# Eight first-table panels beside the making of the gates, and both halves of a route's keys in turn

## The chip, the cores and the metric

One core of one Trainium2 chip runs the whole kernel. The time is that of the device, in microseconds (us), from launch to end; the kernel before takes 3003.77 us, the median of three runs (3003.49 to 3005.74).

## The reference

Two transformer layers over 256 tokens of width 2048, all float32. The first is a convolution block with a SwiGLU; the second has forgetting attention with pooling, and then a layer of 128 x 128 = 16,384 tiny experts (PEER), which is the part that matters here:

```python
def peer(xn, w_query, sub_keys_1, sub_keys_2, expert_u, expert_v):
    q = (xt @ w_query).reshape(t, 8, 256)           # 8 heads
    s1, s2 = q1 . sub_keys_1, q2 . sub_keys_2       # 128 scores each
    v1, i1 = top_k(s1, 16); v2, i2 = top_k(s2, 16)
    cand = v1[..., :, None] + v2[..., None, :]      # 256 pairs
    top_s, top_pos = top_k(cand, 16)
    expert_idx = i1 * 128 + i2 at top_pos; gates = softmax(top_s)
    a = einsum('thkd,td->thk', expert_u[expert_idx], x)
    hid = gelu(a) * gates
    out = einsum('thk,thkd->td', hid, expert_v[expert_idx])
```

So each token takes 8 x 16 = 128 experts, each a row of 2048 floats in the first table (expert_u) and one in the second (expert_v).

## The kernel before

The first 1850 us (convolution, attention, matrix products) are not touched. The expert stage behind them computes the experts in two ways. Experts whose first key is below 88 are **gathered**: a *route* is one head of one half of the tokens (128 tokens, one a partition), 16 routes of 16 slots, in 64 *batches* of four slots. Experts whose first key is one of the last 40 (`DENSE = 40`) are computed **densely**: for each such key a *panel* of 128 experts (1 MB of the first table) is multiplied with all 256 tokens. Its Gelu is kept in `s_ha` (one block a panel), multiplied with gates that are zero where a token didn't choose the expert, and later multiplied with a panel of the second table.

What each engine does in batch g (its loop variable g or i):

- GpSimd issues the gathers, in one order for both tables: first-table row set k, then second-table row set k - 4 (`gather_u` L575, `gather_v` L588). There are 5 buffers for the first table (`s_u`), given back by VectorE's dots, and 7 for the second (`s_v`), given back by TensorE's adding.
- VectorE takes four dots (L1706, two halves each), then sums them (L1718, tile `s_adot`). After dot 0 it multiplies the last batch's activations with their gates (`hidden`, L1752). Batches 0 to 15 but every fifth (4, 9, 14) also carry the work of one route (`route`, L1688): the sixteen best keys of the first half behind dot 0, of the second behind dot 1 (`best_keys`, L1650), the best pairs behind dot 2, the experts' indices behind dot 3. `step` marks an instruction with a semaphore, `settled(back)` waits until all but the last `back` marked ones have ended, `link` does both at once.
- ScalarE makes the Gelu and spreads the activations (`spreads`, L1041) for TensorE, applies the Gelu to finished dense panels (`dense_hidden`, L1054) and, in batches 18 to 31, makes one-key matrices (`one_keys`, L1068).
- TensorE adds up the gathered rows of batch i - 1 (`adds`, L2284) and, in i = 0 to 16, runs the 40 first-table panels (`dense_u_panel`, L2228): three in each of the first two batches and some 2.3 in the others. Panel d goes to bank 4 + d % 4. In i = 18 to 31 it makes the gates, four tokens at a time ("fours", `token_four`, L2264), eight fours in batches 18 and 19 and four in the others, into banks 6 and 7. From i = 34 it runs the second-table panels.
- VectorE multiplies the gates onto `s_ha`, eight tokens of all 40 blocks at a time (`gated`, L1741), two fours behind TensorE.
- SyncE's queue loads the panels into two buffers (L468 to 479), each when the panel two before it is used. At d == DENSE it first waits until all first-table panels are used and then brings back two rows of tiles kept outside (`s_xn_late`, needed by the dots from batch 32 on, and `s_xres_late`, needed by TensorE at i = 33).

## Time and profile before

| | us |
|---|---|
| median of three runs | 3003.77 |
| the profiled execution | 3004.93 |
| its span, first to last instruction | 3002.9 |
| TensorE busy in it | 2736.4 |
| VectorE busy | 1923.8 |
| ScalarE busy | 1178.5 |
| GpSimd busy | 668.0 |

All stretches that are named in the text are in microseconds from the start of the span. PE is TensorE's matrix products, PEld its weight loads, DVE VectorE, ACT ScalarE, POOL GpSimd, SP SyncE. A share of busy time is an average over stages with different limits, so the text goes by stretches of the expert stage, from 1852 us to the end.

### The profile page before, as it was taken

How to read it: one execution, taken by the hardware profiler on the slowest of the kernel's cores; microseconds unless marked ns; L12 is line 12 of the kernel's file. 1: busy time of each engine (PE TensorE's matmuls, PEld its weight loads, DVE VectorE, ACT ScalarE, POOL GpSimd, SP SyncE). 2: the span in 40 equal slices, each digit the busy share in tenths (PEclk: the TensorE clock that was granted, in tenths of full speed). 3: DMA queues.
4: the chain of work that ended last, by engine and by line, in shares of the span. 5: the costliest groups of instructions: out<-in, count | busy, mean ns of one | idle time of the engine just before them, and what ended most of it. 6: DMA issues, size and time to landing. Idle time of an engine off the chain costs nothing.

```text
span 3002.9 us, 45413 instructions
## 1 busy us (share of the span) xinstructions
PE 2736.4 (91%) x17100; PEld 2038.3 (68%) x17100; DVE 1923.8 (64%) x3184; ACT 1178.5 (39%) x2298; POOL 668.0 (22%) x568
## 2 busy tenths in 40 slices
PE   8999999999999998999999999999976678888884
PEld 7886788888888887989999889777753322222220
DVE  6888566555656565455445558987769875555555
ACT  1003443334333344425334444645456642222232
POOL 0000000000000000040000002544448765454453
PEclk9999999999999998999999999999977779999886
DMA  6333545555555553443555657999999999999997
GB/s 244 140 141 111 206 157 185 187 191 183 194 182 193 184 192 122 155 152 141 182 182 182 248 199 250 372 418 408 415 375 408 397 409 417 409 420 391 411 409 300
DMA packets 131297, 785.51 MB, mean 262 GB/s; under 512 B 34630, under 2 KB 34630, under 8 KB 35846
## 3 DMA queue, kind: packets, MB, share of 16 engines
q1 hardware_dynamic: 55424, 393.68, 35.5%
q0 software_dynamic: 75712, 389.74, 32.3%
q8 instruction: 93, 1.52, 0.2%
q14 instruction: 68, 0.56, 0.1%
HBM read 940.23 MB, written 4.19 MB: 315 GB/s over the span
## 4 chain that ended last, share of the span: by engine, by line
PE 57%; DMA 20%; DVE 12%; issue 6%; ACT 3%; POOL 1%; DVEq 1%; POOLq 0%; SPq 0%; ACTq 0%
DMA s_u<-in_expert_u,s_u_index 17%; PE bank L1847 10%; PE bank L1841 10%; PE bank L1843 10%; PE bank L1842 10%; PE bank L1848 5%; PE bank L1937 4%; DVE s_u L1706 4%; PE bank L2240 4%; PE bank L2292 2%; DMA s_v<-in_expert_v,s_v_index 2%; DVE s_cacc L1217 2%; ACT s_spread L1050 2%; DVE s_w_lo L1128 1%; DVE s_yrow L1390 1%
## 5 line engine op out<-in xcount | busy, mean ns | idle before, releaser
L1128 DVE TENSOR_TENSOR s_w_lo<-s_raw,s_w_hi 128x2048 fp32r<-128x2048 f32 x258 | 592.6, 2297 | 577.8 <-ACT s_w_hi L628 577.4
L628 ACT ACTIVATE s_w_hi<-s_raw 128x2048 fp32r<-128x2048 f32 x256 | 490.5, 1916 | 750.9 <-PE bank L1843 475.4
L1847 PE MATMUL bank<-s_a,s_w_hi 128*128 128x512 f32 x1408 | 494.7, 394 | 3.2 <-DVE s_w_lo L1128 3.2
L2292 PE MATMUL bank<-s_v,s_spread 128*32 128x512 f32 x2048 | 302.8, 721 | 183.1 <-ACT s_spread L1050 115.9
L1706 DVE CUSTOM_DVE_ANT_0 s_u<-s_u,s_xn_late 128x1024 f32<-128x1024 f32 x256 | 303.8, 1224 | 246.8 <-DMA s_u<-in_expert_u,s_u_index 246.5
L1050 ACT ACTIVATE s_spread<-s_ident,s_hid 32x32 f32<-32x32 f32 x1024 | 325.6, 318 | 205.5 <-DVE s_hid L1756 188.0
L1848 PE MATMUL bank<-s_a,s_w_lo 128*128 128x256 f32 x1408 | 395.1, 281 | 0.0
L585 POOL DMA_INDIRECT s_u<-in_expert_u,s_u_index x256 | 300.0, 1172 | 416.4 <-DVE s_halfdot L1706 240.4
L601 POOL DMA_INDIRECT s_v<-in_expert_v,s_v_index x256 | 317.9, 1242 | 196.8 <-PE bank L2292 115.5
L1706 DVE CUSTOM_DVE_ANT_0 s_u<-s_u,s_xn 128x1024 f32<-128x1024 f32 x256 | 303.8, 1224 | 60.3 <-DMA s_u<-in_expert_u,s_u_index 59.3
L1841 PE MATMUL bank<-s_a,s_w_hi 128*128 128x256 f32 x1152 | 325.1, 282 | 3.4 <-DVE s_a L1152 1.8
L1842 PE MATMUL bank<-s_a,s_w_hi 128*128 128x256 f32 x1152 | 324.4, 282 | 0.0
L1843 PE MATMUL bank<-s_a,s_w_lo 128*128 128x256 f32 x1152 | 324.0, 281 | 0.0
L2292 PEld LDWEIGHTS bank<-s_v,s_spread 128*32 128x32 f32 x2048 | 62.9, 125 | 375.5 <-ACT s_spread L1050 135.4
L1847 PEld LDWEIGHTS bank<-s_a,s_w_hi 128*128 128x128 f32 x1408 | 264.7, 188 | 66.5 <-DVE s_w_lo L1128 6.4
L2250 PE MATMUL bank<-s_raw,s_ha 128*32 128x512 f32 x2560 | 295.5, 615 | 0.0
L2240 PE MATMUL bank<-s_xnt,s_raw 128*128 128x256 f32 x1184 | 264.7, 382 | 2.1 <-DMA s_raw<-in_dense_u 2.1
L1848 PEld LDWEIGHTS bank<-s_a,s_w_lo 128*128 128x128 f32 x1408 | 265.0, 188 | 0.4
L2240 PEld LDWEIGHTS bank<-s_xnt,s_raw 128*128 128x128 f32 x1184 | 222.1, 190 | 58.7 <-issue 29.1
L1937 PE MATMUL bank<-s_a_f,s_raw 128*128 128x272 f32 x1024 | 235.2, 393 | 2.9 <-DVE s_a_f L1185 2.1
L2250 PEld LDWEIGHTS bank<-s_raw,s_ha 128*32 128x32 f32 x2560 | 83.3, 115 | 215.1 <-issue 215.1
L1937 PEld LDWEIGHTS bank<-s_a_f,s_raw 128*128 128x128 f32 x1024 | 194.4, 190 | 43.4 <-issue 3.5
(321 smaller groups left out, 3809.8 us busy)
## 6 DMA issues: line engine op xcount, KB each, us to landing
s_raw<-in_stream SPq DMA_DIRECT2D x292, 1024.0 KB, 4.7
s_raw<-in_expert_v SPq DMA_DIRECT2D x40, 1024.0 KB, 8.9
s_raw<-in_dense_u SPq DMA_DIRECT2D x37, 1024.0 KB, 8.7
s_u<-in_expert_u,s_u_index POOLq DMA_INDIRECT x256, 17.4
s_v<-in_expert_v,s_v_index POOLq DMA_INDIRECT x256, 17.6
s_panel_early<-in_dense_u POOLq DMA_DIRECT2D x3, 1024.0 KB, 11.5
s_xres<-in_x SPq DMA_DIRECT2D x2, 1024.0 KB, 6.0
out<-s_out_row SPq DMA_DIRECT2D x32, 64.0 KB, 3.3
```

The costliest lines, as they stand in the source:

```text
L628: act.activation(w_hi[s % 2][:, :], raw[s][:, :], ACT.Copy).then_inc(hi_ready, 1)
L1050: ins = act.activation(spread[g % NW][s * Q:(s + 1) * Q, q, :], ident[own, own], ACT.Copy, scale=hid[g % NH][own, s:s + 1])
L1128: dve.tensor_tensor(w_lo[s % 2][:, :], raw[s][:, :], w_hi[s % 2][:, :].bitcast(f32), ALU.subtract)\
L1706: ins = dve.tensor_tensor_reduce(out=u_slot[k % NU][:, half], in0=u_slot[k % NU][:, half], in1=xn_late[:, half] if t else xn[:, 0, half], ...
L1841: pe.matmul(dst, left[0], right[0], start=start, stop=False)
L1842: pe.matmul(dst, left[0], right[1], start=False, stop=False)
L1843: return pe.matmul(dst, left[1], right[0], start=False, stop=stop)
L1847: pe.matmul(dst, left[0], both, start=start, stop=False)
L1848: return pe.matmul(dst[:, 0:T], left[1], both[:, 0], start=False, stop=stop)
L1937: ins = pe.matmul(bank[c][:, 0:L], raw[c % 4][:, k * 128:(k + 1) * 128], a_f[:, k, :], start=k == 0, stop=k == KT - 1)
L2240: ins = pe.matmul(bank[b][:, 0:T], source[:, k * 128:(k + 1) * 128], xnt[:, k, 0:T], start=k == 0, stop=k == KT - 1)
L2292: ins = pe.matmul(bank[4 * t + q][c * Q:(c + 1) * Q, :], spread[g % NW][:, q, :], v_slot[k % NV][:, c * 512:(c + 1) * 512], start=False, s ...
```

## The change

Of the forty first-table panels 32 (`FIRST_U`) pass in batches 0 to 16, one or two in each from the first on, and 8 (`LATE_U`) while the gates are made: panel 32 at i = 18, then one each at i = 20, 21, 23, 25, 26, 28 and 29, at the head of TensorE's work of the batch. They use banks 4 and 5. A late panel misses the gates of the tokens before it. So `gated` copies the gates of the missing blocks into `s_ha` as they are; ScalarE puts the Gelu of the tokens already gated into a new tile (`s_late_act`, on the place of `s_pick` and `s_cand`, which the routes no longer need) and that of the others into `s_ha`; and VectorE multiplies the two in a new step, `landed`, two batches after the panel (batches 20, 22, 23, 25, 27, 28, 30, 31, with 48 to 224 tokens). SyncE's code is the same, but its wait for all forty panels now ends at i = 29.

The keys of both halves of a route are found behind dot 0 with their instructions in turn (`best_keys_of_both`), so that a step waits for one that is not the last. The pairs move behind dot 1, the indices behind dot 2.

```diff
+FIRST_U, LATE_U = 32, 8
...
-    return d + 16 if d < 24 else d - 16 if d < 32 else d - 32
+    return d + 16 if d < 24 else d - 16 if d < FIRST_U else DENSE - 1 - d
...
 def u_panels_in(i):
 
-    if i < 2:
-        return range(3 * i, 3 * i + 3)
-    return range(6 + 34 * (i - 2) // 15, 6 + 34 * (i - 1) // 15) if i < 17 else range(0)
+    if i < 17:
+        return range(FIRST_U * i // 17, FIRST_U * (i + 1) // 17)
+    return range(FIRST_U + LATE_U * (i - 17) // 13, FIRST_U + LATE_U * (i - 16) // 13) if i < 30 else range(0)
+
+
+def u_bank(d):
+
+    if d < FIRST_U:
+        return 4 + d % 4, d // 4
+    return 4 + (d - FIRST_U) % 2, FIRST_U // 4 + (d - FIRST_U) // 2
+
+
+def gated_before(g):
+
+    fours = 8 * (g - 18) if g < 20 else 4 * (g - 16)
+    return max(0, min(fours, T // 4) // 2 - 2)
+
+
+LANDS_IN = {d: i + 2 for i in range(30) for d in u_panels_in(i) if d >= FIRST_U}
...
+    late_act = place("s_late_act", [128, 2, T], pick_at)
...
             def dense_hidden(d):
 
-                b = 4 + d % 4
+                b, late = u_bank(d)[0], d - FIRST_U
                 act.wait_ge(panel_used, NPANELS + 1 + d + 1)
-                if d == 32:
-                    act.wait_ge(expert_ready, PH)
-                act.activation(ha[:, dense_block(d), :], bank[b][:, 0:T], ACT.Gelu_apprx_tanh).then_inc(bank_empty[b], 1)
+                done = 0
+                if late >= 0:
+                    done = GATE_TOKENS * gated_before(LANDS_IN[d])
+                    if late == 0:
+                        act.wait_ge(expert_ready, TT * PH)
+                    wait(act, late_landed, late - 1)
+                    act.activation(late_act[:, late % 2, 0:done], bank[b][:, 0:done], ACT.Gelu_apprx_tanh)
+                act.activation(ha[:, dense_block(d), done:], bank[b][:, done:T], ACT.Gelu_apprx_tanh).then_inc(bank_empty[b], 1)
...
+            def best_keys_of_both(th):
+
+                values = [val[:, half * TOPK:(half + 1) * TOPK] for half in range(2)]
+                indices = [ind[:, half * TOPK:(half + 1) * TOPK] for half in range(2)]
+                src = [score[:, score_row(th), half * NKEYS:(half + 1) * NKEYS] for half in range(2)]
+                rest = [sc_rest[:, :], cand_rest[:, 0:NKEYS]]
+                for h in range(2):
+                    apart()
+                    step(dve.max(values[h][:, 0:8], src[h]))
+                for h in range(2):
+                    settled(1 + h)
+                    apart()
+                    step(dve.max_index(indices[h][:, 0:8], values[h][:, 0:8], src[h]))
+                    step(dve.match_replace(rest[h], values[h][:, 0:8], src[h], LOWEST))
+                for h in range(2):
+                    settled(2 - h)
+                    apart()
+                    step(dve.max(values[h][:, 8:16], rest[h]))
+                for h in range(2):
+                    settled(1)
+                    apart()
+                    step(dve.max_index(indices[h][:, 8:16], values[h][:, 8:16], rest[h]))
+                settled()
...
             def route(th, turn):
 
-                if turn < 2:
-                    best_keys(th, turn)
+                if turn == 0:
+                    best_keys_of_both(th)
+                elif turn == 1:
+                    best_pairs()
                 elif turn == 2:
-                    best_pairs()
-                else:
                     pairs_experts(th)
...
-            def gated(group):
+            def gated(group, missing):
 
                 b = 6 + group % 2
                 if group == 0:
                     for a in range(2):
-                        dve.wait_ge(bank_empty[4 + a], n.after(f"empty{4 + a}", DENSE // 4))
+                        dve.wait_ge(bank_empty[4 + a], n.after(f"empty{4 + a}", FIRST_U // 4))
                 dve.wait_ge(one_key_used, GATE_TOKENS // 4 * (group + 1))
                 some = ha[:, :, GATE_TOKENS * group:GATE_TOKENS * (group + 1)]
-                dve.tensor_tensor(some, some, bank[b][:, 0:GATE_TOKENS * DENSE].rearrange("p (t g) -> p g t", t=GATE_TOKENS), ALU.mult)\
-                    .then_inc(bank_empty[b], 1)
+                gates = bank[b][:, 0:GATE_TOKENS * DENSE].rearrange("p (t g) -> p g t", t=GATE_TOKENS)
+                if missing:
+                    dve.tensor_copy(some[:, 0:missing, :], gates[:, 0:missing, :])
+                dve.tensor_tensor(some[:, missing:, :], some[:, missing:, :], gates[:, missing:, :], ALU.mult).then_inc(bank_empty[b], 1)
+
+            def landed(d):
+
+                late, (b, k) = d - FIRST_U, u_bank(d)
+                groups = gated_before(LANDS_IN[d])
+                for group in (groups - 2, groups - 1):
+                    gates_taken = n.after(f"empty{6 + group % 2}", FIRST_U // 4 + 2 + group // 2)
+                    dve.wait_ge(bank_empty[6 + group % 2], gates_taken)
+                dve.wait_ge(bank_empty[b], n.after(f"empty{b}", k + 1))
+                some = ha[:, dense_block(d), 0:GATE_TOKENS * groups]
+                dve.tensor_tensor(some, some, late_act[:, late % 2, 0:GATE_TOKENS * groups], ALU.mult).then_inc(late_landed, 1)
...
-                    fours = token_fours_in(g)
+                    for d in range(FIRST_U, DENSE):
+                        if turn == 0 and LANDS_IN[d] == g:
+                            landed(d)
+                    fours, missing = token_fours_in(g), sum(LANDS_IN[d] > g for d in range(FIRST_U, DENSE))
                     for f in fours[turn * len(fours) // 4:(turn + 1) * len(fours) // 4]:
                         if f >= 4 and f % 2 == 0:
-                            gated(f // 2 - 2)
+                            gated(f // 2 - 2, missing)
...
             def dense_u_panel(d):
 
-                b = 4 + d % 4
+                b, k = u_bank(d)
                 if d == 0:
                     pe.wait_ge(xnt_ready, 1)
-                into(b, d // 4)
+                into(b, k)
```

Counts of buffers' uses (`DENSE // 4` becomes `FIRST_U // 4`, and for banks 4 and 5 at i = 33 `FIRST_U // 4 + LATE_U // 2`) follow in the same way.

## Rows read from the trace of the kernel before

**Rows 1.** the page's parts 2 and 3: DMA tenths, GB/s in 40 slices, gathers' queue

```profile
DMA  6333545555555553443555657999999999999997
GB/s 244 140 141 111 206 157 185 187 191 183 194 182 193 184 192 122 155 152 141 182 182 182 248 199 250 372 418 408 415 375 408 397 409 417 409 420 391 411 409 300
...
q0 software_dynamic: 75712, 389.74, 32.3%
```

**Rows 2.** windows: length, busy us (instructions) by engine, granted clock, DMA share, GB/s

```profile
1852.00:1912.00 60.00, 57.62 (x292) 45.26 (x282) 54.44 (x160) 26.93 (x87) 22.18 (x21) 1.00 0.84 305
1912.00:2186.00 274.00, 272.49 (x1445) 198.19 (x1444) 222.10 (x615) 152.44 (x490) 134.39 (x112) 1.00 1.01 414
2186.00:2251.00 65.00, 46.49 (x273) 32.15 (x271) 43.52 (x81) 32.23 (x96) 28.03 (x25) 0.74 0.92 371
2251.00:2450.00 199.00, 134.61 (x890) 68.18 (x893) 179.48 (x337) 118.44 (x358) 148.53 (x112) 0.73 1.00 402
2450.00:2985.00 535.00, 423.13 (x3527) 111.40 (x3519) 294.93 (x543) 158.82 (x510) 272.27 (x237) 0.88 0.99 405
1960.00:1980.00 20.00, 20.00 (x108) 14.65 (x107) 18.20 (x55) 12.16 (x40) 10.14 (x9) 1.00 1.02 424
```

**Rows 3.** waits, 1852 to 2200 us: total us, times, longest

```profile
POOL s_v L601 <- PE bank L2292: 80.6, 25, 9.8
...
DVE s_u L1706 <- DMA s_u<-in_expert_u,s_u_index: 39.1, 20, 3.9
```

**Rows 4.** groups by line, 1852 to 2200 us: count | busy, mean ns | idle before

```profile
L2240 PE MATMUL bank<-s_xnt,s_raw 128*128 128x256 f32 x1184 | 264.7, 382 | 2.1 <-DMA s_raw<-in_dense_u 2.1
...
L2292 PE MATMUL bank<-s_v,s_spread 128*32 128x512 f32 x512 | 61.6, 598 | 1.8 <-ACT s_spread L1050 1.8
```

**Rows 5.** timeline of DVE: sums that end batches 2, 3 and 4; start, duration in us

```profile
1911.78 0.15 DVE L1718 TENSOR_TENSOR s_adot<-s_halfdot 128x4 f32<-128x4 f32 x1
...
1931.85 0.15 DVE L1718 TENSOR_TENSOR s_adot<-s_halfdot 128x4 f32<-128x4 f32 x1
...
1941.83 0.17 DVE L1718 TENSOR_TENSOR s_adot<-s_halfdot 128x4 f32<-128x4 f32 x1
```

**Rows 6.** timeline of DVE: one half of a route's keys before, start and duration

```profile
1894.74 0.29 DVE L1639 MAX8 s_val<-s_score 128x8 f32<-128x128 f32 x1
1895.18 0.09 DVE L1641 MATCH_VALUE_LOAD s_ind<-s_val,s_score 128x8 f32 x1
1895.26 0.28 DVE L1641 FIND_INDEX8 s_ind<-s_val,s_score 128x8 uint32<-128x128 f32 x1
1895.46 0.07 DVE L1642 MATCH_VALUE_LOAD s_sc_rest<-s_val,s_score 128x8 f32 x1
...
1896.78 1.22 DVE L1706 CUSTOM_DVE_ANT_0 s_u<-s_u,s_xn 128x1024 f32<-128x1024 f32 x1
```

**Rows 7.** timeline of PE: fours (L2280) and adding (L2292), idle time in brackets

```profile
2216.85 3.71 PE L2280 MATMUL bank<-s_one_key,s_one_key 128*128 128x40 f32 x16 [12.63 <-ACT s_one_key L1082]
...
2223.90 5.50 PE L2292 MATMUL bank<-s_v,s_spread 128*32 128x512 f32 x32
...
2245.79 4.80 PE L2292 MATMUL bank<-s_v,s_spread 128*32 128x512 f32 x32
...
2285.16 5.59 PE L2292 MATMUL bank<-s_v,s_spread 128*32 128x512 f32 x32 [4.21 <-ACT s_spread L1050]
2290.68 1.98 PE L2280 MATMUL bank<-s_one_key,s_one_key 128*128 128x40 f32 x16
```

**Rows 8.** DMA issues and median landing: 1852:1912, 1945:2186, 2345:2450

```profile
s_u<-in_expert_u,s_u_index POOLq DMA_INDIRECT x12, 8.6
...
s_u<-in_expert_u,s_u_index POOLq DMA_INDIRECT x48, 19.9
...
s_u<-in_expert_u,s_u_index POOLq DMA_INDIRECT x29, 14.9
```

**Rows 9.** groups by line and shape, 2186 to 2450 us

```profile
L1749 DVE TENSOR_TENSOR s_ha<-s_ha,bank 128x320 f32<-128x320 f32 x32 | 15.4, 481 | 3.2 <-PE bank L2280 3.2
```

More of the change, by code:

```diff
@@ L442, in two_layers @@
         spread_ready, v_used = sem("spread_ready"), sem("v_used")
+        late_landed = sem("late_landed")
         acc_done, out_ready, stored = sem("acc_done"), sem("out_ready"), sem("stored")
@@ L1082, in one_keys @@
                 act.activation(four, four, ACT.Relu, scale=-1.0, bias=1.0).then_inc(one_key_ready, 1)
-            slots_stored = [n.after(f"empty{6 + t}", DENSE // 4 + 1) for t in range(TT)]
+            slots_stored = [n.after(f"empty{6 + t}", FIRST_U // 4 + 1) for t in range(TT)]
             for g in range(ROUTES * GROUPS):
@@ L1723, in one_keys_2 @@
                     for t in range(TT):
-                        dve.wait_ge(bank_empty[6 + t], n.after(f"empty{6 + t}", DENSE // 4 + 1))
+                        dve.wait_ge(bank_empty[6 + t], n.after(f"empty{6 + t}", FIRST_U // 4 + 1))
                 wait(dve, one_key_used, 2 * (m - 2))
@@ L1815, in _ @@
                     if g == 32 and turn < 2:
-                        gated(T // GATE_TOKENS - 2 + turn)
+                        gated(T // GATE_TOKENS - 2 + turn, 0)
                 dots_summed(g)
@@ L2258, in slots_transposed @@
                 pe.wait_ge(gates_ready, PH * (t + 1))
-                into(6 + t, DENSE // 4)
+                into(6 + t, FIRST_U // 4)
                 for kind in range(3):
@@ L2267, in token_four @@
                 if f % 2 == 0:
-                    into(b, DENSE // 4 + 1 + f // 4)
+                    into(b, FIRST_U // 4 + 1 + f // 4)
                 turn = 2 * (f // 4) + f % 4
@@ L2309, in _ @@
                     for b in (4, 5):
-                        into(b, DENSE // 4)
+                        into(b, FIRST_U // 4 + LATE_U // 2)
                     for b in (6, 7):
-                        into(b, DENSE // 4 + 1 + T // GATE_TOKENS // 2)
+                        into(b, FIRST_U // 4 + 1 + T // GATE_TOKENS // 2)
                     pe.wait_ge(xres_back, 16)
```

## Prediction

> **What bounds the kernel now.** I read the page first: the DMA's busy tenths and rate over time, and what the gathers moved [rows 1]. The change touches only the last part of the kernel, the expert stage, which starts near 1852 us. There the DMA row stands at 9 in nearly every slice and the rate near 410 GB/s. So the stage is first of all bound by bytes; the question is where the DMA engines are *not* full. Second, I cut the stage into five stretches [rows 2]. The last column is the rate (five rows; the sixth is one window of 20 us): 305 GB/s in the first 60 us (the first three batches), 414 up to 2186, 371 while the one-key machinery starts, 402 while the gates are made, 405 after that. Times the lengths this is 18.3, 113.4, 24.1 and 80.0 MB for the first four. Third, the waits of the first two stretches [rows 3]: VectorE waited 39.1 us for gathered rows of the first table, and the queue of GpSimd, which issues all gathers in order, waited 80.6 us for TensorE to give back buffers of the second table. TensorE's work there is 37 first-table panels in 264.7 us, 7.15 us each, with hardly any idle time in front (2.1 us), three more like them, and 61.6 us of adding, 3.85 a batch [rows 4]: 40 x 7.15 + 61.6 = 348 us, all there is from 1852 to 2200. So up to batch 16 TensorE and the DMA are both full. The first batches have a third limit: the sums of two routed batches lie 20.07 us apart (1911.78, 1931.85), the next, without a route, takes 9.98 [rows 5], and a gather lands in 8.6 us against 19.9 later [rows 8]: VectorE sets the pace and the DMA has room. While the gates are made a gather takes 14.9 us [rows 8]: nearly full, not quite.
>
> **The profiled execution** spans 3002.9 us and took 3004.93; the median is 3003.77. I change the profiled stretches and take the difference from the median.
>
> **The change, part by part.**
>
> *Alternating the halves.* Before, each half of a route's keys is a chain in which every step but one waits for the instruction just before it: four waits a half, eight a route. From the first maximum (1894.74) to the next dot (1896.78) one half takes 2.04 us [rows 6]; two take 4.08. An instruction behind a wait starts 0.15 us after the end of the one before (0.29 us from 1894.74, then 1895.18); one without a wait starts 0.08 before it (1895.46 against 1895.54) [rows 6]. After the change seven of the eight waits look one or more instructions further back. At 0.23 each I walk the new order to about 2.65 us for both halves, 1.4 saved per route; bounds are 0 (the waits aren't what holds it) and 1.6. A routed batch then costs VectorE 18.7 us instead of 20.07. Only where VectorE sets the pace does this shorten the kernel: three batches in the first stretch, 3 x 1.4 = **4.2 us** (0 to 4.8). Pairs and experts move one dot earlier; the indices are used batches later, nothing there is late.
> The row shows 0.23 us between a waiting and a free instruction. The Trainium skill ("VectorE: DVE Perf Modes", the section on the DRAIN you can't avoid) says that the next operation starts only when the pipeline is empty and that the semaphore costs nothing extra, so that only the number of operations counts. By that rule alternation saves nothing; that is a rival below. The trace disagrees, with starts 0.08 us ahead of the end.
>
> *Eight panels leave the first 17 batches.* TensorE loses 8 x 7.15 = 57 us of work there and is no longer the limit. Per five batches (four routed) it then has 9.4 x 7.15 + 5 x 3.85 = 86 us, VectorE 4 x 18.7 + 10 = 85, so the DMA should lead. Loads run two panels ahead, so by the end of batch 16 they are at panel 33 instead of 39: six loads of 1.05 MB fewer, two of them in the first stretch (where the DMA isn't the limit), four in the second. 113.4 - 4.2 = 109.2 MB. At which rate? 414 GB/s was reached beside a TensorE that held buffers back; single windows reach 424 [rows 2]. I take 418: 261 us instead of 274, **13 us** saved. Bounds: 405 GB/s, the rate of the last stretch [rows 2], gives 270 (4 saved), 422 gives 259 (15). The first batches get one or two panels instead of three; their adding waits for ScalarE's copies, not for TensorE, and TensorE idles some microseconds, which costs nothing there.
>
> *Batches 17 to 19.* SyncE's queue loads the two rows kept outside (tile xn_late and xres_late) and the first two second-table panels once all forty panels are used. That was at the start of this stretch, 4.2 MB in 10 us of DMA time; now it comes after panel 39, in batch 29. One or two late panels (1.0 MB) take its place: 24.1 - 4.2 + 1.0 = 20.9 MB, 50 us at 414. VectorE has 43.5 us here [rows 2] plus about 1.5. What else bounds it is the chain sum, spread, one-keys, eight fours, adding: 21.9 us for batch 19 with hardly a wait for gathers in it (adding starts at 2223.90, 2245.79) [rows 7]. Batch 17 has 389.7/64 = 6.1 MB of gathers [rows 1], 15.5 us. With two batches of 20 to 21 behind it this is 57 us for 65, **8 us** saved (bounds 4 and 13, the latter with VectorE and DMA alone). Panel 32 stands ahead of the first fours of batch 18, in the 12.63 us in which TensorE waited for ScalarE [rows 7]: free, as long as that wait is longer than the panel. VectorE has gates only for those landed; the chain isn't longer.
>
> *The gates, batches 20 to 33.* Added on VectorE: 28 small copies and 8 products of 48 to 224 columns. Neither is in the trace; the copies move 8 to 64 elements a row, between the 155 ns of a four-column sum [rows 5] and the 481 ns of the 320-column gate product [rows 9]. Near the lower end: 28 x 0.17 + 8 x 0.28 = 7 us, less 1.5 for the shorter gate products, 5.5 (bounds 3 and 12). VectorE had 179 of 199 us; 185 stays under what the DMA needs. The waits in front of a landing are for instructions a batch old. ScalarE: two Gelu instead of none, 0.8 us a panel beside 118 us in 199. The DMA: 80.0 + 4.2 (moved here) + 5.2 (five late panels) = 89.4 MB. At 402, the present rate, 222 us; at 422, 212. The present rate is one of 12 slots in flight with no plain loads beside them; with loads beside them the gathers took 19.9 us and the rate was 414 [rows 2, 8], so I take 415: 215.4 us instead of 199, **16.4 us** lost (bounds 13 and 23). The loads moved here are due at batch 32 (xn_late), three batches after the issue, some 40 us against a landing of at most 20 [rows 8].
> TensorE: seven panels stand ahead of the adding, which now waits 4.2 us for ScalarE [rows 7]. A panel of 7.15 us passes 2.9 us on. Behind it the GpSimd queue stands with a gather of the second table, and behind that the next gather of the first, which VectorE needs. With 14.9 us in flight, I expect 2.9 us to be covered.
>
> *After batch 33* nothing is changed: same bytes, same order, same panels in hand.
>
> **Sum:** -4.2 - 13 - 8 + 16.4 = -8.8 us: **2995 us**. Best ends together: -4.8 - 15 - 13 + 13 = -20; worst: 0 - 4 - 4 + 23 = +15.
>
> **Rivals.**
> *The alternation gives nothing* (the drain rule). Routed batches stay at 20.07: the first stretch saves nothing, the second has 10 x 20.07 + 4 batches of some 16 = 265, 9 saved. -9 - 8 + 16.4 = -0.6, **3003 us**. Against it: the overlapping starts in [rows 6].
> *Bytes alone.* The same megabytes are moved; where the gates are made the DMA runs at 402 again (+23), the rest as forecast: -2, **3002 us**. For it: a DMA share of 1.00 at 402 [rows 2].
> *The DMA never starves.* Panels fill the weak stretches, rates of 422 in both long stretches, and batches 17 to 19 in 53 us: -4.2 - 15 - 12 + 13 = -18, **2986 us**. For it: 371 and 305 GB/s are there to be filled.
> *TensorE becomes the bound while the gates are made (slower).* Its granted clock is 0.73 on average in that stretch [rows 2], between the levels of 1.2 and 2.4 GHz, as it idles 4 us in every batch; the same adding takes 5.59 us there [rows 7] against 3.85 [rows 4]. If the panels run at 1.2 GHz, 14.3 us each, TensorE has 14 x 9.4 (adding and fours, [rows 7]) + 7 x 14.3 = 232 us, over the 215 of the DMA: +32 instead of +16.4, **3011 us**. It decides when the seven panels take more than (215 - 132)/7 = 12 us each. Against it: the panels fill just the idle time before which the clock fell, and the fours, which run right behind the adding, have full speed (1.98 us for 16 [rows 7], 3.71 after a gap).
> The Trainium skill ("TensorE: Matmul & The Clock Gate", Part 1) says that an idle TensorE falls to half clock and a busy one returns; the trace agrees with it, and it speaks on both sides: for slow panels behind a gap, against gaps once they are filled.
>
> **How the numbers follow.** Forecast 0.42; alternation empty 0.17; bytes alone 0.10; never starving 0.17; TensorE bound 0.14. What a measurement of this kernel can tell from no change is about 0.2%, 6 us, so faster means under 2997.8. The forecast's own spread (2989 to 3001) lies on that side with 0.36 of its 0.42; with the never-starving case 0.53 faster. The two middle rivals and the rest of the forecast are 0.33 same; 0.14 slower. The range leaves out the outer part of the best and of the slower case: 2984 to 3008.
>
> **What would show it.** Right: sums of the first routed batches 18.7 us apart; the dot of batch 16 ending near 2168; TensorE with some 8% idle before that; a rate of 415 or more in the gate stretch and its end (sum of batch 33) at about 2441 instead of 2450; panels of about 7.2 us there. Wrong: routed batches still 20 us apart; gather times under 15 us between 1930 and 2168 (then something else than the DMA holds it); GpSimd waiting long for TensorE between 2226 and 2441; the first dots of batch 32 waiting for xn_late.

## The result: 10 us slower

| | before | after |
|---|---|---|
| median, seven runs each in turn | 3005.16 us | 3015.01 us |
| lowest to highest | 3003.49 to 3008.86 | 3012.25 to 3017.70 |
| span of the profiled execution | 3002.9 | 3013.0 |

After over before: 1.0034, 95% interval 1.0025 to 1.0044. Forecast were 2995 us and a range of 2984 to 3008; the kernel is slower by more than the 0.2% that can be told.

The page of the kernel after: span, granted clock, DMA tenths, GB/s in 40 slices of the span.

```profile
span 3013.0 us, 45458 instructions
...
PEclk9999999999999999999999999999988778998886
DMA  6343545555555553444545657999989999999997
GB/s 243 140 141 111 209 154 188 188 183 193 183 193 183 193 181 130 154 147 143 186 181 182 250 196 255 370 415 408 412 330 419 385 417 417 411 420 394 413 407 303
```

Against [rows 1]: where batches 17 to 19 run there is now a slice of 330 GB/s (before 375). The same five stretches as [rows 2], cut at the same events (the ends of VectorE's sums of batches 2, 16, 19 and 33); columns as there: length, busy us of PE, PEld, DVE, ACT, POOL, granted clock, DMA share, GB/s.

```profile
1852.00:1908.00 56.00, 41.95 (x206) 30.56 (x199) 53.10 (x159) 26.05 (x83) 20.69 (x20) 0.85 0.77 275
1908.00:2174.00 266.00, 250.04 (x1301) 174.06 (x1300) 216.82 (x615) 150.39 (x484) 122.21 (x112) 0.96 1.01 412
2174.00:2238.00 64.00, 48.16 (x266) 32.26 (x268) 43.69 (x88) 32.33 (x97) 30.91 (x25) 0.76 0.86 334
2238.00:2461.00 223.00, 180.32 (x1132) 112.77 (x1128) 183.27 (x367) 121.72 (x372) 143.15 (x112) 0.80 0.99 401
2461.00:2996.00 535.00, 423.22 (x3528) 110.75 (x3520) 295.45 (x548) 159.16 (x512) 266.01 (x237) 0.88 0.99 406
```

The ends of the last three sums that cut it (line, tile, start, duration):

```profile
2173.93 0.16 DVE L1766 TENSOR_TENSOR s_adot<-s_halfdot 128x4 f32<-128x4 f32 x1
...
2237.83 0.16 DVE L1766 TENSOR_TENSOR s_adot<-s_halfdot 128x4 f32<-128x4 f32 x1
...
2461.05 0.16 DVE L1766 TENSOR_TENSOR s_adot<-s_halfdot 128x4 f32<-128x4 f32 x1
```

Every kernel of this study was cut in the same way. All later sections read from this table; a time is the length of the stretch in that kernel's trace, "rest" runs to the end of its span, and the last two columns are of timed runs, 5 to 11 of each (the kernel before, timed beside them, took 3004.3 to 3005.5 us). One of its runs took 4581.89 us at a granted clock of 0.554 and is in no median or ratio here. Each kernel has one trace, and the seven that are the same program up to batch 16 (after, late_no_loads, spread_loads, late_two, fours_half, panels_behind, panels_last) end that batch between 2173.1 and 2176.0: 2 or 3 us in one stretch can be chance.

| kernel | up to batch 2, ends at | batches 3 to 16 | 17 to 19 | 20 to 33 | rest | median | ratio, 95% |
|---|---|---|---|---|---|---|---|
| before | 1911.8 | 273.7 | 65.2 | 199.3 | 552.9 | 3005.16 | |
| after | 1907.5 | 266.4 | 63.9 | 223.2 | 552.0 | 3015.01 | 1.0034 (1.0025–1.0044) |
| keys_only | 1907.4 | 275.7 | 64.7 | 199.7 | 553.4 | 3004.07 | 0.9996 (0.9987–1.0005) |
| panels_only | 1912.3 | 261.7 | 64.8 | 221.9 | 552.5 | 3015.89 | 1.0034 (1.0021–1.0048) |
| before_late_loads | 1912.0 | 272.1 | 63.7 | 209.1 | 553.3 | 3012.20 | 1.0026 (1.0016–1.0036) |
| late_no_loads | 1907.2 | 266.2 | 62.9 | 210.2 | 554.0 | 3002.51 | 0.9990 (0.9981–0.9999) |
| spread_loads | 1907.9 | 266.0 | 63.9 | 221.7 | 555.0 | 3016.48 | 1.0036 (1.0023–1.0050) |
| late_two | 1907.2 | 265.9 | 64.6 | 222.2 | 550.5 | 3013.01 | 1.0027 (1.0016–1.0037) |
| fours_half | 1909.9 | 266.1 | 58.7 | 222.6 | 551.0 | 3008.78 | 1.0009 (1.0000–1.0018) |
| front_loaded | 1907.7 | 260.7 | 66.2 | 223.1 | 552.1 | 3013.19 | 1.0028 (1.0016–1.0040) |
| even40 | 1910.6 | 276.5 | 68.0 | 199.4 | 553.5 | 3010.39 | 1.0017 (1.0008–1.0026) |
| two_in_gap | 1908.6 | 272.2 | 68.6 | 199.9 | 552.1 | 3003.27 | 0.9994 (0.9985–1.0003) |
| panels_behind | 1907.7 | 266.5 | 63.3 | 222.9 | 555.2 | 3019.71 | 1.0050 (1.0036–1.0063) |
| panels_last | 1907.8 | 266.7 | 61.6 | 225.7 | 554.2 | 3018.29 | 1.0046 (1.0032–1.0059) |

So the sum that was forecast as -4.2 - 13 - 8 + 16.4 = -8.8 came out as -4.3 - 7.3 - 1.3 + 23.9 - 0.9 = +10.1 us. Three terms missed by some 6 to 8 us each, all to the same side.

### The profile page after: what moved, and what is told of

Same layout as the page of the kernel before. It is cut to its first block, busy times and chain, and to the rows that moved or that the text cites. A ratio compares the mean times of both kernels' runs of the same rounds, so it can differ in the third digit from the quotient of the medians.

```text
span 3013.0 us, 45458 instructions
## 1 busy us (share of the span) xinstructions
PE 2745.7 (91%) x17100; PEld 2043.8 (68%) x17100; DVE 1921.4 (64%) x3220; ACT 1179.0 (39%) x2306; POOL 645.9 (21%) x568
## 4 chain that ended last, share of the span: by engine, by line
PE 59%; DMA 19%; DVE 11%; issue 5%; ACT 4%; DVEq 1%; POOL 1%; POOLq 0%; SPq 0%; ACTq 0%
DMA s_u<-in_expert_u,s_u_index 16%; PE bank L1911 10%; PE bank L1905 10%; PE bank L1906 10%; PE bank L1907 10%; PE bank L1912 5%; PE bank L2001 4%; PE bank L2304 4%; DVE s_u L1754 3%; PE bank L2356 3%; DMA s_v<-in_expert_v,s_v_index 3%; PE bank L2314 2%; DVE s_cacc L1241 2%; ACT s_spread L1069 2%; PE bank L2344 1%
## 5 line engine op out<-in xcount | busy, mean ns | idle before, releaser
L604 POOL DMA_INDIRECT s_u<-in_expert_u,s_u_index x256 | 290.4, 1134 | 505.3 <-DVE s_halfdot L1754 318.4
L620 POOL DMA_INDIRECT s_v<-in_expert_v,s_v_index x256 | 305.3, 1193 | 140.3 <-issue 76.9
L2304 PE MATMUL bank<-s_xnt,s_raw 128*128 128x256 f32 x1184 | 271.5, 388 | 0.0
L2304 PEld LDWEIGHTS bank<-s_xnt,s_raw 128*128 128x128 f32 x1184 | 226.5, 194 | 58.0 <-issue 27.6
## 6 DMA issues: line engine op xcount, KB each, us to landing
s_panel_early<-in_dense_u POOLq DMA_DIRECT2D x3, 1024.0 KB, 11.6
```

The costliest lines, as they stand in the source:

```text
L2304: ins = pe.matmul(bank[b][:, 0:T], source[:, k * 128:(k + 1) * 128], xnt[:, k, 0:T], start=k == 0, stop=k == KT - 1)
```

## The experiments

The theories at stake: the *bytes* decide where the gates are made (a moved load costs its DMA time), or TensorE's work, or where that work stands; and in batches 17 to 19 a *chain* of engines decides and loads ride along for nothing, or the bytes do.

### One half of the change alone

**keys_only** is the kernel before with the new keys.

```diff
-                if turn < 2:
-                    best_keys(th, turn)
+                if turn == 0:
+                    best_keys_of_both(th)
+                elif turn == 1:
```

> The kernel before with the alternation alone; all forty panels stay in the first 17 batches. Theory A (TensorE sets the first 17 batches there, VectorE only the first three): the first batches' sums lie 18.7 us apart instead of 20.07, but the stretch to batch 16 ends where it did (2185, within 2 us), as TensorE's 348 us of work are untouched; total 3005, within 3 us. Rival: the alternation is worth its full 4.2 us or more on its own: sum of batch 16 at 2181 or earlier, total 3001 or less.

**panels_only** is the kernel after with the old keys (this edit the other way).

> The changed kernel with the keys of a route in the old order (half after half, each instruction waiting for the last). If the alternation shortens every routed batch that TensorE no longer sets: sums of routed batches 20.1 us apart throughout, batch 16 ends at 2179 to 2182 instead of 2174, total 3019 to 3023. Rival (the DMA sets the stretch after 1930, so only the first batches lose): batch 16 ends at 2177 to 2179, total 3016 to 3019. If the drain rule held and the waits cost nothing: no change, 3014 to 3016.

Measured: 3004.07 and 3015.89 us. The loss is all the panels'. The new keys are as fast as forecast: VectorE of the kernel after, one route (start, duration):

```profile
1872.86 0.49 DVE L1688 MAX8 s_val<-s_score 128x8 f32<-128x128 f32 x2
1873.30 0.09 DVE L1692 MATCH_VALUE_LOAD s_ind<-s_val,s_score 128x8 f32 x1
...
1874.35 0.29 DVE L1697 MAX8 s_val<-s_sc_rest 128x8 f32<-128x128 f32 x1
1874.58 0.29 DVE L1697 MAX8 s_val<-s_cand_rest 128x8 f32<-128x128 f32 x1
1874.79 0.08 DVE L1701 MATCH_VALUE_LOAD s_ind<-s_val,s_sc_rest 128x8 f32 x1
...
1875.44 1.23 DVE L1754 CUSTOM_DVE_ANT_0 s_u<-s_u,s_xn 128x1024 f32<-128x1024 f32 x1
```

Both halves take 1875.44 - 1872.86 = 2.58 us instead of 4.08 [rows 6]: 1.5 saved (1.4 forecast). Yet keys_only ends batch 2 4.4 us early and then takes 2.0 us more for batches 3 to 16, ending batch 16 at 2183.1 instead of 2185.5; with the panels moved as well nothing of it is left at batch 16, 2174.0 without it and 2173.9 with it. Its timed gain, 0.9996, can't be told from none.

panels_only came out as neither of its first two theories: it ends batch 16 at 2174.0, not at 2177 or later, and the total is that of "no change", though for another reason than the one given there, since the keys do take longer. Where the time goes is seen in the batches. Batches 11 to 13, with a route each, take 60.5 us in it and 56.3 in the kernel after; batch 14, without one, takes 12.1 in it and 18.7 after. What VectorE saves in routed batches it waits in the next one. And up to batch 2 panels_only had moved 60 x 0.267 = 16.0 MB where the kernel after had moved 56 x 0.275 = 15.4.

### Loads moved into the gates, and loads taken out of them

**before_late_loads** is the kernel before, except that SyncE holds back the four plain loads behind the panels (4.2 MB) until batch 27 has been added up; nothing else moves.

```diff
                     sp.wait_ge(panel_used, NPANELS + 1 + DENSE)
+                    sp.wait_ge(v_used, 4 * 28)
```

> The kernel before, but the four loads of 1.05 MB (the two rows kept outside and the first two second-table panels) wait until the adding of batch 27 is done, as they in effect do in the changed kernel. Theory L (these loads were free at batches 17 to 19, where the chain of one-keys, fours and adding sets the pace and the DMA has room, and cost their DMA time where the gates are made): batches 17 to 19 take 62 to 65 us instead of 65, batches 20 to 33 take 207 to 211 instead of 199, total 3011 to 3015: the whole loss of the change. Rival (late panels alone do the harm): batches 17 to 19 gain what the others lose, total within 3 us of 3005.

**late_no_loads** is the kernel after without the loads of the last six late panels (6.3 MB, 5.8 of them where the gates are made, by the windows below); TensorE multiplies what lies in the buffers, so the result is another. (The count of loads that the second-table panels wait for follows.)

```diff
+                if FIRST_U + 2 <= d < DENSE:
+                    continue
...
-                else:
+                elif d < FIRST_U + 2:
                     pe.wait_ge(raw_loaded[(d - NE) % 2], (NPANELS // 4 + (d - NE) // 2 + 1) * 16)
```

> The changed kernel without the loads of its last six late panels (TensorE multiplies what lies in the buffers, so the result is another; all instructions stay). Theory bytes: 6.3 MB fewer, one load of them at batches 17 to 19 (no gain there: the chain sets the pace) and five where the gates are made, at 2.4 us each: batches 20 to 33 take 209 to 213 us instead of 223, total 3001 to 3005. Theory TensorE or VectorE (the panels' work, not their bytes): within 3 us of 3015.

**late_two** is the kernel after with the loads, but only 2 of 16 products of each late panel.

```diff
-                for k in range(KT):
+                for k in range(KT) if d < FIRST_U else (0, KT - 1):
```

> The changed kernel, with each of the eight late panels multiplied in 2 steps of 16 instead of all (part of the sum is left out): TensorE has 0.9 us of work for such a panel instead of 7.15, all transfers and all work of the other engines stay. If the panels ahead of the adding do the harm, because the adding gives buffers back late and the queue of GpSimd stands (theory TensorE): batches 20 to 33 take 212 to 216 us instead of 223, total 3004 to 3008. If bytes set that stretch (theory bytes): 221 to 224, total 3013 to 3016.

Windows of batches 17 to 19 and 20 to 33 of the three, in this order, columns as above:

```profile
2184.00:2248.00 64.00, 47.89 (x277) 33.20 (x275) 43.58 (x84) 32.33 (x97) 30.67 (x26) 0.76 0.83 323
2248.00:2457.00 209.00, 140.66 (x888) 71.22 (x891) 180.09 (x338) 118.56 (x358) 146.36 (x112) 0.70 1.00 403
```

```profile
2173.00:2236.00 63.00, 46.49 (x262) 30.08 (x261) 43.66 (x88) 32.35 (x97) 30.18 (x24) 0.78 0.85 322
2236.00:2446.00 210.00, 178.61 (x1112) 115.63 (x1112) 182.48 (x368) 121.76 (x372) 148.11 (x112) 0.81 0.99 398
```

```profile
2173.00:2238.00 65.00, 41.06 (x230) 25.76 (x232) 43.85 (x90) 32.47 (x98) 30.48 (x25) 0.71 0.84 329
2238.00:2460.00 222.00, 158.44 (x928) 86.39 (x924) 183.41 (x368) 121.60 (x372) 142.75 (x112) 0.71 1.00 403
```

The second line of each gives the megabytes: 209 x 0.403 = 84.2, 210 x 0.398 = 83.6, 222 x 0.403 = 89.5; before it was 80.0 and after 223 x 0.401 = 89.4. Time follows bytes, at 398 to 403 GB/s, and nothing else in these lines: late_no_loads does all the work of the kernel after on every engine and takes 13 us less; late_two takes 22 us off TensorE (158 for 180) and gets 1 us, and 2 us in all. All three stretches lie where the theories of bytes had put them (207 to 211, 209 to 213 and 221 to 224 us). Four loads cost before_late_loads 9.8 us there (2.45 each) and some 7 us in all; without six of them the kernel after is 12.5 us faster.

The first line of each tells the second thing. The kernel before moved 24.1 MB in this stretch and took 65.2 us; before_late_loads moved 64 x 0.323 = 20.7 MB and took 63.7. Taking 3.4 MB away saved 1.5 us, which is within chance, and not the 8.5 that they would take at 402 GB/s.

### Is it the burst, or where the panels stand?

**spread_loads** lets the four loads go one after another instead of together behind panel 39.

```diff
+                    sp.wait_ge(v_used, 4 * 30)
...
+                if d >= DENSE and d < DENSE + 2:
+                    sp.wait_ge(v_used, 4 * (31 + d - DENSE))
```

(The first stands before the load of xres_late.)

> The changed kernel, with the four loads no longer issued at once behind panel 39 but the first at once and the others one a batch from the adding of batch 29 on. If it is their coming in one burst that starves the dots and the adding near 2400 (theory burst): batch 30 takes 15 to 16 us instead of 21.2 and the total falls by 4 to 8 us to 3007 to 3011. If their bytes are what costs (theory bytes): batches 30 to 34 share the same loss, total 3013 to 3017.

No gain: 221.7 us there, but 3 us more in the rest, 3016.48 in all. Batch 30 does fall from 21.2 to 13.7 us, as the theory of the burst has it, but batch 29 grows from 17.1 to 21.5 and batches 32 and 33 by 4.4 together: the bytes' time only moves.

Next, one place in the kernel after fitted the forecast's own warning sign, GpSimd waiting for TensorE. GpSimd's issues (start, duration, idle time before and who ended it):

```profile
2375.11 1.10 POOL L604 DMA_INDIRECT s_u<-in_expert_u,s_u_index  x1 [0.30 <-issue]
2381.13 1.99 POOL L620 DMA_INDIRECT s_v<-in_expert_v,s_v_index  x1 [4.92 <-PE bank L2356]
```

TensorE had begun the panel ahead of that batch's adding at 2369.84, and the DMA's rate over 2370 to 2400, in 40 slices, shows the hole:

```profile
GB/s 372 426 426 350 371 306 415 339 295 361 361 350 350 372 186 186 109 66 197 251 448 284 262 295 339 371 393 437 415 361 426 295 426 393 404 426 371 481 371 459
```

It falls to 66 GB/s near 2383 us, and the mean of these 30 us is 344. **panels_behind** puts the late panels of batches 20 to 29 behind the adding, **panels_last** behind the fours too.

```diff
-                for d in u_panels_in(i)[:1]:
+                for d in u_panels_in(i)[:1] if i < 20 else ():
                     dense_u_panel(d)
...
-                for d in u_panels_in(i)[2:]:
+                for d in u_panels_in(i)[2 if i < 20 else 0:]:
                     dense_u_panel(d)
```

> The kernel after, with the seven late panels of batches 20 to 29 behind TensorE's adding of their batch and ahead of its fours, instead of ahead of both. The computation is whole. In the trace of the kernel after the rate falls from some 420 GB/s to 66 to 250 between 2379 and 2385 us, right behind a late panel of 9.41 us (2369.84), while GpSimd waits 4.92 us for TensorE to give back a buffer of the second table; from 2370 to 2400 the rate is 344 GB/s. Theory A (a late panel at the head of TensorE's work holds buffers back, and that is the missing rate): the dip is gone, GpSimd's waits for TensorE between 2238 and 2461 (17.3 us in the kernel after) fall, the stretch of batches 20 to 33 takes 223 - 5 = 218 us, total near 3010. Theory B (the bytes set the end, a dip is made up by the buffers in hand or by others elsewhere): the stretch stays at 222 to 223 us, total 3013 to 3016. Theory C (the fours are now late, and VectorE's gate products wait for them): over 225 us.

> As the kernel panels_behind, with the late panels of batches 20 to 29 behind the fours of their batch, so that neither the adding nor the fours of the batch wait for them; a panel can hold only the next batch's adding, which waits for ScalarE's copies in any case. The computation is whole. Theory A: 217 to 218 us for batches 20 to 33, total near 3009 to 3010, and no dip of the rate under 300 GB/s near 2380. Theory B: 222 to 223 us, total 3013 to 3016, the same as panels_behind. Theory C: under panels_behind by what its gate products waited for TensorE.

Neither is faster: 3019.71 and 3018.29 us, read as slower than the kernel after by 3 to 5, though the intervals of the ratios overlap. No theory had the totals right; the stretch of panels_behind is that of theory B (222.9 us), the one of panels_last is over B's and A's (225.7). The hole moves: the rate of panels_behind falls to 142 GB/s near 2394, that of panels_last to 229 near 2400. The waits of panels_behind between 2238 and 2465 (total us, times, longest):

```profile
POOL s_u L604 <- PE bank L2356: 27.7, 7, 7.3
...
DVE s_ha L1799 <- PE bank L2344: 25.7, 8, 6.5
```

The same of the kernel after, 2238 to 2461:

```profile
POOL s_u L604 <- PE bank L2356: 9.6, 6, 5.6
POOL s_v L620 <- PE bank L2356: 7.7, 4, 4.9
DVE s_ha L1799 <- PE bank L2344: 6.9, 5, 3.0
```

GpSimd waits for TensorE 27.7 us in front of the first table's gathers (after 17.3 in front of both tables'), and VectorE 25.7 us for gates (after 6.9). So these two runs put other waits in the place of the first, and what the hole itself costs they can't show. The stretch takes 222.9 us again with 88.4 MB (89.3 after), and the rest is 3 us longer.

late_two shows it, because there the panel at the head is nearly gone. Its rate over the same 30 us, 2370 to 2400:

```profile
GB/s 437 382 415 426 339 317 350 393 382 382 404 339 459 317 426 361 306 361 317 361 306 371 339 382 437 393 459 393 404 437 382 459 415 448 393 448 426 404 448 404
```

No slice is under 306 GB/s and the mean is 391, yet the stretch takes 222.2 us for 223.2. The hole is gone and the time isn't: the theory that the place at the head costs the missing rate falls.

### What bounds batches 17 to 19

**fours_half** is the kernel after with the products of two of the four tokens in each of the first sixteen fours (those of batches 18 and 19), so half of these gates are left out.

```diff
-                for e in range(4):
+                for e in ((0, 3) if f < 16 else range(4)):
```

> The changed kernel with two of four tokens in each of the first sixteen fours (batches 18 and 19; half of these gates are left out). Theory chain (batches 17 to 19 are set by sum, spread, one-keys, fours, adding, one behind the other, the first fours at half clock): TensorE's 7.3 + 3.9 us of fours a batch are halved, batches 18 and 19 take 19 to 21 us instead of 23.7 and 22.4, together 4 to 8 us less, and total 3008 to 3012. Rival (VectorE's own work or the gathers set them): within 2 us of 3015.

TensorE of the kernel after in this stretch (start, duration, idle before):

```profile
2192.72 7.17 PE L2304 MATMUL bank<-s_xnt,s_raw 128*128 128x256 f32 x32
...
2225.84 3.71 PE L2344 MATMUL bank<-s_one_key,s_one_key 128*128 128x40 f32 x16 [6.31 <-ACT s_one_key L1106]
2229.35 3.61 PE L2344 MATMUL bank<-s_one_key,s_one_key_late 128*128 128x40 f32 x16
2232.90 6.09 PE L2356 MATMUL bank<-s_v,s_spread 128*32 128x512 f32 x32
```

TensorE waits 6.31 us for ScalarE's one-keys, then runs 16 small products in 3.71 us where 1.98 is its time at full clock [rows 7]; the granted clock of the stretch is 0.76, a mean of its two levels, 1.2 and 2.4 GHz. (The Trainium skill, "TensorE: Matmul & The Clock Gate", Part 1, has a TensorE that sat idle at half clock; the row agrees.) Behind them stands the adding, and GpSimd waits for it, 15.8 us in this stretch. The same stretch of fours_half (columns as above):

```profile
2176.00:2235.00 59.00, 37.99 (x214) 22.02 (x212) 43.67 (x88) 32.49 (x98) 33.18 (x25) 0.80 0.92 358
```

With half of these products it takes 58.7 us instead of 63.9 (batches 18 and 19: 21.2 and 19.8 for 23.7 and 22.4), at 358 GB/s instead of 334 and nearly the same bytes, and the kernel 3008.78 us instead of 3015.01: the chain over these engines sets this stretch, and time taken out of it reaches the end. Batch 19 shows the chain most plainly: it takes 22.41 or 22.42 us in all nine kernels with late panels and whole fours, and 21.81 to 21.89 in before, keys_only and before_late_loads. The half microsecond between them fits ScalarE's two Gelu of the late panel, which stand right ahead of its one-keys in the kernel after (2223.33 to 2223.78); that was not tried by itself.

The room has an end. even40 and two_in_gap (below) move 26.3 and 25.7 MB in this stretch and take 68.0 and 68.6 us. Whether bytes cost that, or in two_in_gap the two panels, was not tried.

### How the first seventeen batches share the panels

**front_loaded** is the kernel after with three panels in each of the first two batches, as before, and 26 in the others.

```diff
+    if i < 2:
+        return range(3 * i, 3 * i + 3)
     if i < 17:
-        return range(FIRST_U * i // 17, FIRST_U * (i + 1) // 17)
+        return range(6 + 26 * (i - 2) // 15, 6 + 26 * (i - 1) // 15)
```

> The changed kernel with three panels again in each of the first two batches and 26 spread over the next fifteen; the eight late panels stay. Theory free room (before about 1930 the DMA isn't full because VectorE sets the pace, so the loads drawn there are free, and the even distribution gives two of them up): the stretch up to batch 16 has 2.1 MB less to move when the DMA is full, batch 16 ends at 2168 to 2171 instead of 2174, total 3009 to 3013. Rival (the sum of bytes up to batch 16 alone decides, wherever they lie): batch 16 at 2173 to 2175, total 3014 to 3016.

**even40** is the kernel before with its forty panels spread evenly.

```diff
-    if i < 2:
-        return range(3 * i, 3 * i + 3)
-    return range(6 + 34 * (i - 2) // 15, 6 + 34 * (i - 1) // 15) if i < 17 else range(0)
+    return range(DENSE * i // 17, DENSE * (i + 1) // 17) if i < 17 else range(0)
```

> The kernel before with its forty panels spread evenly over the first 17 batches (two or three in each), nothing late, keys in the old order. Theory TensorE (it sets that stretch with 348 us of work, and every gap it gets in the first two batches moves the end): it runs out of panels before the adding of batch 1 and idles 5 to 8 us, batch 16 ends at 2189 to 2194 instead of 2185, total 3009 to 3013. Rival (the DMA alone sets that stretch): batch 16 within 2 us of 2185, total 3003 to 3007.

The first two stretches of front_loaded:

```profile
1852.00:1908.00 56.00, 55.18 (x280) 43.61 (x276) 53.05 (x159) 26.91 (x86) 18.98 (x19) 1.00 0.84 303
1908.00:2168.00 260.00, 233.98 (x1223) 158.28 (x1216) 216.31 (x613) 149.75 (x482) 123.94 (x113) 0.93 1.00 409
```

It moves 303 GB/s in the first 56 us, where the kernel after moves 275: 1.6 MB more, in the same time. Batch 16 ends 5.5 us earlier (2168.4 against 2173.9). Of that 2.3 us go again in batches 17 to 19 (66.2 for 63.9), and 3013.19 is only 1.8 under 3015.01, which their intervals don't tell apart: batch 16 ended where theory free room had it, the total did not. even40 loses 5 to 6 us on before (1.0017): batch 16 ends 1.6 us later, where the rival had it, and batches 17 to 19 take 2.8 more, so that the total is the one of theory TensorE. TensorE, which has the same forty panels to do up to batch 16, sits idle 8.64 us early on for want of ScalarE's copies (in the kernel before 1.76, at 1882.48). That this is what costs it was not tried by itself.

```profile
1881.25 3.64 PE L2290 MATMUL bank<-s_v,s_spread 128*32 128x512 f32 x16 [8.64 <-ACT s_spread L1048]
```

### Only what fits the gap

**two_in_gap** moves two panels instead of eight, to batches 17 and 18, where TensorE waits for ScalarE, and keeps three in each of the first two batches (panel 38 stands behind the adding of i = 17). It has the new keys.

```diff
-FIRST_U, LATE_U = 32, 8
+FIRST_U, LATE_U = 38, 2
...
+    if i < 2:
+        return range(3 * i, 3 * i + 3)
     if i < 17:
-        return range(FIRST_U * i // 17, FIRST_U * (i + 1) // 17)
-    return range(FIRST_U + LATE_U * (i - 17) // 13, FIRST_U + LATE_U * (i - 16) // 13) if i < 30 else range(0)
+        return range(6 + 32 * (i - 2) // 15, 6 + 32 * (i - 1) // 15)
+    return range(21 + i, 22 + i) if i < 19 else range(0)
```

(The counts of buffers' uses follow.)

> Another distribution, with the alternation: 38 panels in the first 17 batches, three in each of the first two as before, one behind the adding of batch 17 and one at the head of batch 18, in the 12.6 us in which TensorE waits for the one-keys. The four loads of kept rows and second-table panels then follow at about 2215, still where the DMA has room. Theory free room: nothing is moved to where the gates are made, TensorE has 14 us less before; the first 17 batches end 3 to 6 us earlier than 2185, the rest stays: total 2998 to 3002, faster than the kernel before. Rival (the DMA's bytes up to batch 16 are the same 37 loads, so nothing is gained): 3003 to 3006.

Measured 3003.27 us, ratio 0.9994 with 1 inside its interval: the total of the rival, not the 2998 to 3002 of theory free room. It wins 4.7 us up to batch 16 (2180.8 for 2185.5), loses 3.4 in the next three (68.6 for 65.2), and pays nothing in the gates. It beats the kernel after by 12 us and the kernel before by nothing that can be told.

## Why the prediction was wrong, step by step

**The alternation, -4.2.** Right in its own place (-4.3; routed batches end 18.69 us apart, 1869.83 and 1888.52, for 18.7). The rival that it saves nothing is refuted, and with it the reading of the drain rule that the prediction weighed (the Trainium skill, "VectorE: DVE Perf Modes", The DRAIN you can't avoid): 2.58 us for 4.08, with as many instructions. (The same section of the Trainium skill adds that an operation that isn't held starts earlier; the row agrees, with 1895.46 against an end at 1895.54 [rows 6].) The step that failed is the sum: the gain of the first three batches was added to the one of batches 3 to 16, as if the second began where the first ended. Between 1852 us and batch 16 the kernel after moves 56 x 0.275 + 266 x 0.412 = 125.0 MB at 388 GB/s over the whole; getting through the first batches sooner takes time from the DMA in which it had room, and it is paid behind them. panels_only, without the alternation, ends batch 16 at the same time: the term is worth nothing in this sum, 4.8 us gained in front (1907.5 for 1912.3) and 4.7 lost behind (266.4 for 261.7).

**Eight panels leave batches 3 to 16, -13.** The mechanism holds and the size was off: -7.3, or together with the first term -11.6 for -17.2. The bytes were as reckoned, 266 x 0.412 = 109.6 MB for 109.2. The rate was 412 instead of 418, and 109.6/0.418 would have been 262 us: this is 4 us of the miss. In no kernel of this study was the stretch above 415 GB/s; that TensorE, which held buffers back, kept the rate down was an assumption, and with that wait shorter (GpSimd for TensorE, 1852 to 2200: 92.2 us before, 30.6 after) the rate did not rise. The prediction rightly took the two loads fewer in the first stretch as no gain, but did not use the room: front_loaded puts them back and gains 5.5 us at batch 16. TensorE is indeed no limit there: busy 250 of 266 us, 6% idle for the 8% named; VectorE still waited 39.6 us for gathers.

**Batches 17 to 19, -8: the step that failed by its mechanism.** The prediction named both limits, bytes and the chain, and then let four loads fewer shorten the stretch to 57 us: 15.5 for batch 17, the time of its gathers' bytes, and 20 to 21 for each of the two behind it, though its own row had 21.9 for batch 19 with hardly a wait for gathers. The three take 17.7, 23.7 and 22.4 us after and 17.5, 25.8 and 21.9 before. Taking the four loads away saves 1.5 us (before_late_loads) and halving the fours 5.2: the chain is the limit, so the loads that the change moved away had cost next to nothing where they were (1.5 us of 8.5, within chance). This was to be read from [rows 2], where the stretch ran at 371 GB/s and a share of 0.92 with TensorE at 0.74 of its clock.

**The gates, +16.4: a term mis-sized.** The bytes were right, 89.4 MB. The rate was not: 401, not the 415 that I took from a stretch with more plain loads; 89.4/0.401 = 223 us. The step that failed is that plain loads beside the gathers would lift the rate: with nine of them it is 401, with four 403 (before_late_loads), with none 402 [rows 2]. All twelve other kernels stayed between 393 and 403 whatever was done to TensorE, to the order of panels or to the moments of the loads; the lowest is panels_last. The rival "bytes alone" had this term right (+23 for +23.9). Its total of 3002 missed for the other two terms. The VectorE work added did not decide: busy 183 us in 223, late_no_loads has all of it and takes 210. Its price was 166 to 222 ns a copy and 202 to 427 a landing, some 8 us in all for the 7 estimated.

**TensorE, the slower rival.** 3011 us is near the time, but by accident. The panels did not run at half clock (at L2304, 2174 to 2461 us; the row also holds the end of panel 31):

```profile
L2304 PE MATMUL bank<-s_xnt,s_raw 128*128 128x256 f32 x280 | 64.8, 391 | 0.0
```

Seven of the eight late panels took 7.15 to 7.17 us and one, at 2369.84, 9.41: a mean of 7.4, not 14.3. The clock of the stretch rose from 0.73 to 0.80; and late_two, with nearly all that work gone, takes 222.2 us.

**Right besides:** panel 32 is free for TensorE in the gap of batch 18 (7.17 us ending at 2199.9, and the stretch isn't longer), though "the chain isn't longer" was wrong by the half microsecond of batch 19; no wait of an engine for xn_late shows in the trace; after batch 33 nothing changes (552.0 for 552.9).

Put together: eight panels out of batches 0 to 16 gain 11 to 12 us. Some 9.4 MB more pass where the gates are made, at 2.4 to 2.7 us for each load of 1.05 MB (9.8/4, 23.9/9): +24. What left batches 17 to 19 for it had been all but free.

**Open:** why the rate of the gate stretch stays near 400 GB/s at a DMA share of 0.99 while batches 3 to 16 reach 406 to 415 over all kernels. A small part lies at its start, where the DMA comes out of the chain of batch 19 nearly empty: in the kernel after 28 GB/s in the 5 us ahead of 2238, then 272 and 369 in the first two stretches of 5 us (before 128 ahead of 2251, then 297 and 377). Behind them, after and before:

```profile
2248.00:2461.00 213.00, 170.32 (x1064) 104.25 (x1066) 173.77 (x350) 114.14 (x349) 135.52 (x107) 0.79 0.99 404
2261.00:2450.00 189.00, 128.93 (x852) 64.42 (x848) 169.51 (x319) 110.92 (x335) 141.71 (x107) 0.73 1.01 406
```

The burst and TensorE's work are not it, and no other place of the panels raised it. That the two stretches differ in the mix of gathers and plain loads wasn't tried alone.

## What to carry to other kernels

A moved transfer has two prices: what it frees where it leaves, which is next to nothing if a chain of other engines sets the pace there, and what it costs where it lands, its bytes at the rate that this very stretch shows. Before moving work away from a full engine, look for what rides along with it, such as loads queued behind it that had a free place. And of two gains in front of the same limit only one counts; check each by how much the limiting resource still has to do at the end of the stretch.

## What the runs showed of the hardware

A load of 1.05 MB in a stretch with a DMA share of 0.99 to 1.00 costs nearly its bytes in time (2.6 us at 403 GB/s): 9.8 us for four in that stretch (before_late_loads) and 13.0 for 5.8 MB (late_no_loads), 2.4 each. A hole in the DMA's rate, 344 GB/s over 30 us, looked like the cause and wasn't: without it (late_two, 391 over the same 30 us) the stretch was 1 us shorter. And two independent chains of short, dependent VectorE instructions, taken in turn, cost 2.58 us where one after the other they cost 4.08, their instructions starting 0.21 and 0.23 us apart (1874.35, 1874.58, 1874.79) where behind a wait it is 0.44 (1894.74, 1895.18 [rows 6]).
